# Feed-forward with Strassen products: VectorE's work reordered and paired, the convolution on one stretch, and the low part of one weight sum made by GpSimd

## The reference

```
def conv_ffn(h, p, buf):
    u = h @ p['w_ffn_up']
    a, v = u[..., :D_FF], u[..., D_FF:]          # D_FF = 2816
    T = a.shape[1]
    ext = jnp.concatenate([buf.astype(a.dtype), a], axis=1)
    w = p['ffn_conv_w']
    c = p['ffn_conv_b'] + sum(ext[:, j:j + T] * w[j] for j in range(CONV_W))   # CONV_W = 3
    out = (jax.nn.silu(c) * v) @ p['w_ffn_down']
    return out, ext[:, -(CONV_W - 1):]
```

## Time and profile before

| what | value |
|---|---|
| median of three runs | 1988.31 us |
| the profiled execution | 1987.89 us, of which the span is 1986.1 us |
| PE busy | 1825.2 us (92%) |
| DVE busy | 1313.5 us (66%) |
| ACT busy | 962.6 us (48%) |
| POOL busy | 242.9 us (12%) |
| mean granted clock of PE | 0.985 |

### The profile page before, as it was taken

One profiled execution on the slowest core, in us unless ns is written; L12 is line 12 of the kernel. 1 busy time (PEld: TensorE's weight loads), 2 busy tenths in 40 slices (PEclk: granted clock), 3 DMA queues, 4 the chain that ended last, 5 costly groups with the idle time before them and its releaser, 6 DMA issues.

```text
span 1986.1 us, 31514 instructions
## 1 busy us (share of the span) xinstructions
PE 1825.2 (92%) x11636; PEld 1658.3 (83%) x11636; DVE 1313.5 (66%) x2229; ACT 962.6 (48%) x1601; POOL 242.9 (12%) x261
## 2 busy tenths in 40 slices
PE   8999999998889999898899999999988989898985
PEld 7999965798888889897799999658988989798974
DVE  5777865437675666677777778653575675757776
ACT  6444455437544343535654444653555353534345
POOL 0000034001111111111000001430011111111100
PEclk9999999999899999999999999999999999999998
DMA  5211231411646565555131123132135556555621
GB/s 189 72 55 66 68 89 46 131 54 49 152 123 138 144 145 131 133 154 123 43 107 55 52 72 80 63 118 68 65 84 132 133 131 150 131 140 150 139 69 59
DMA packets 98713, 203.71 MB, mean 103 GB/s; under 512 B 16800, under 2 KB 35616, under 8 KB 98536
## 3 DMA queue, kind: packets, MB, share of 16 engines
q1 hardware_dynamic: 63760, 144.06, 22.6%
q0 software_dynamic: 21888, 39.86, 12.3%
q10 hardware_dynamic: 12912, 17.78, 2.7%
HBM read 170.65 MB, written 8.65 MB: 90 GB/s over the span
## 4 chain that ended last, share of the span: by engine, by line
PE 58%; DVE 21%; ACT 10%; DMA 5%; issue 4%; DVEq 0%; POOL 0%; ACTq 0%; SPq 0%; POOLq 0%
PE G L768 36%; PE WA L768 12%; PE WB L768 8%; DVE tmp L2100 6%; DVE wlo L2100 4%; ACT tmp L1453 3%; DMA t<-in_wstream 3%; DVE ax L2100 2%; DVE Y L2100 2%; DMA wraw<-in_wstream 1%; PE G L772 1%; ACT sq L1453 1%; DVE gl L2100 1%; ACT Y L1453 1%; PE WB L772 1%
## 5 line engine op out<-in xcount | busy, mean ns | idle before, releaser
L768 PE MATMUL G<-Hh,wlo 128*128 128x328 f32 x1384 | 456.8, 330 | 56.5 <-DVE p L2100 32.5
L768 PE MATMUL G<-Hh,whi 128*128 128x328 f32 x1384 | 436.8, 316 | 0.0
L768 PE MATMUL G<-Hl,whi 128*128 128x328 f32 x1384 | 435.8, 315 | 0.0
L768 PEld LDWEIGHTS G<-Hh,wlo 128*128 128x128 f32 x1384 | 264.3, 191 | 76.5 <-DVE p L2100 40.2
L768 PEld LDWEIGHTS G<-Hh,whi 128*128 128x128 f32 x1384 | 264.6, 191 | 2.3 <-issue 0.4
L768 PEld LDWEIGHTS G<-Hl,whi 128*128 128x128 f32 x1384 | 263.8, 191 | 0.0
L1453 ACT ACTIVATE whi<-wraw 128x1024 fp32r<-128x1024 f32 (+2 forms) x194 | 160.3, 826 | 184.2 <-PE G L768 113.2
L2100 DVE TENSOR_TENSOR wlo<-wraw,whi 128x1024 fp32r<-128x1024 f32 (+2 forms) x194 | 181.7, 936 | 45.1 <-ACT whi L1453 28.2
L768 PE MATMUL G<-gh,wlo 128*128 128x328 f32 x424 | 136.1, 321 | 23.5 <-DVE tmp L2100 17.1
L2100 DVE SCALAR_TENSOR_TENSOR tmp<-ax,cols,tmp 128x528 f32<-128x528 f32 (+1 forms) x176 | 98.6, 560 | 57.9 <-ACT tmp L1453 51.8
L768 PE MATMUL G<-gh,whi 128*128 128x328 f32 x424 | 134.5, 317 | 0.0
(11 more groups left out here) (326 smaller groups left out, 4135.1 us busy)
## 6 DMA issues: line engine op xcount, KB each, us to landing
wraw<-in_wstream SPq DMA_DIRECT2D x108, 512.0 KB, 3.3
wff<-in_wstream SPq DMA_DIRECT2D x40, 512.0 KB, 4.7
t<-in_wstream SPq DMA_DIRECT2D x76, 256.0 KB, 4.1
t<-in_wstream POOLq DMA_DIRECT2D x38, 256.0 KB, 5.5
ckT<-in_ckT SPq DMA_DIRECT2D x12, 512.0 KB, 3.4
wff<-in_wstream POOLq DMA_DIRECT2D x20, 256.0 KB, 4.2
t<-wff POOLq DMA_DIRECT2D x20, 256.0 KB, 3.3
wff<-t POOLq DMA_DIRECT2D x20, 256.0 KB, 3.3
```

The source lines that it names most:

```text
L768: return pe.matmul(out, lhsT, rhs, start=start, stop=stop, skip_group_check=True)
```

## The change

- The order of splits: `LATE` is changed, and where two units in neighbouring places are split behind the same product (`PAIRS`: B11 with B21, T2 with T3, T4 with B22), ACT and DVE do both in one instruction of 1024 columns. `t2` and `t3` become one tensor `t23` for that. `ring` is as before, so some pairs stay two instructions.
- The low part of T1 is made by POOL (`t1_low`), behind `sum_t4` of its chunk and ahead of `sum_t1` of the next. It has its own semaphore, `t1_split`; `split_sem` tells PE and SP which of the two to wait for.
- The convolution works in its own tensor `cc` on one stretch of 672 columns with one instruction per tap. The silu now goes from `cc` to `tmp` in two. `cc` takes the place of `cos4`, which is loaded again in layer 1. `halo` and `carry` go from DVE to ACT.
- In a chunk, DVE does `conv_rest` ahead of most splits, and splits T2 with T3 of the next chunk ahead of the addition to `u2`, which leads to `ax`.
- The first stage of the feed-forward: `token_sums` of POOL is gone; the sums are made by DVE (20 instructions of 328 columns, `s_sum`) and ACT in `Sf`. The weights of the fifth and sixth tile are split earlier; part of the sums, and the high part of the last of them, move behind the start of the first down pass.
- The end of a layer: the first weights of the next layer are split before the last halves, and the second halves of outputs 3 and 4 come behind the first residuals.

```
-LATE = {B11: 0, B21: 0, T2: 2, T3: 1, T1: 1, T4: 1, B22: 0}
+LATE = {B11: 1, B21: 0, T2: 1, T3: 0, T1: 0, T4: 1, B22: 0}
+PAIRS = (B11, T2, T4)
...
+        def pair_of(g):
+            k = product_of(g % UNITS_L)
+            return k is not None and k[1] in PAIRS and ring[g + 1] == ring[g] + 1 and \
+                any(g % UNITS_L in v and g % UNITS_L + 1 in v for v in split_after.values())
+        def split_at(g):
+            l, u = divmod(g, UNITS_L)
+            before = l * NS + sum(u0 + T1 <= u for u0 in U_PROD.values())
+            return ("t1_split", before) if by_pool(g) else ("w_split", g + 1 - before)
...
@@ POOL
+            def t1_low(l, c):
+                g = unit_of(chunk_no(l, c), T1)
+                pool.wait_ge(S("w_hi"), g + 1)
+                pool.tensor_tensor(w_lo_of(g), raw_unit(g), w_hi_of(g), ALU.subtract).then_inc(S("t1_split"), 1)
...
-                token_sums(l)
                 sum_t1(l, NPL)
                 sum_t2(l, NPL)
                 for c in range(NPL, KF):
                     sum_t3(l, c)
                     sum_t4(l, c)
+                    t1_low(l, c)
                     if c + 1 < KF:
                         sum_t1(l, c + 1)
                         sum_t2(l, c + 1)
@@ ACT
                 def conv_first(c):
-                    act.wait_ge(S("conv"), 2 * k + 1)
...
-                    step(f(d[:, 0:PT], s_[:, 0:PT], ACT.Identity, **kw))
-                    did(f(samples(d[:, PT:T]), samples(s_[:, 2 + PT:EXT], DT + 2)[:, :, 0:DT], ACT.Identity, **kw), "silu")
+                    act.wait_ge(S("ax"), l * KF + c + 1)
+                    did(f(cc[:, 0:EXT - 2], ax[:, c % 2, 0:EXT - 2], ACT.Identity, scale=cols[:, l, C_CW + c:C_CW + c + 1],
+                          bias=cols[:, l, C_CB + c:C_CB + c + 1]), "silu")
...
@@ ACT, first down pass
                     for n in range(KD):
                         if not q:
                             act.wait_ge(S("down"), down_no(l, q, n))
-                            act.wait_ge(S("s_dve"), s_split(l, 1 if n < KH else 3))
                             did(f(two(Y[:, n, :]), halves(down_bank(n)), ACT.Copy), "act_took")
+                        if not q and n == 3:
+                            s_high(Sh[:, 0, :, :], Sf[:, 0, :, :], 18)
+                            act.wait_ge(S("tile"), t0 + T_UP + 2 * NPL)
+                            for x in range(2):
+                                s_high(Hh[:, 2 * x:2 * x + 2, cols_of(1)], s4_part(x), 12, -1.0)
@@ DVE, chunk
+                    lows(l, u0 - 2)
                     if pending is not None:
                         conv_rest(pending)
-                    lows(l, u0 - 2)
-                    halo(c)
-                    lows(l, u0 - 1)
+                    lows(l, u0 + B11)
                     after(B21)
...
-                    lows(l, u0 + B11)
                     if pending is not None:
                         times_v(pending)
-                    lows(l, u0 + B21)
+                    lows(l, u0 + T2)
                     if pending is not None:
                         g_low(pending)
-                    lows(l, u0 + T2)
                     after(T1)
                     did(tt_(p7[:, :], p7[:, :], bank(G[s], 0), ALU.add), "dve_took")
-                    lows(l, u0 + T3)
+                    lows(l, u0 + T1)
                     after(T4)
...
-                    carry(c)
-                    lows(l, u0 + T1)
@@ DVE, end of a layer
                 split_to[0] = 0
+                w_low(l + 1, 0)
...
-                for n in (3, 4):
-                    ffn_out_b(n)
-                for n in (3, 4):
-                    add_square_b(n0 + N_FFNPOST, n)
+                ffn_out_b(3)
                 dve.wait_ge(S("rstd_a"), 2 * l + 2)
```

More of the change, by code:

```diff
@@ L609, in _ @@
                 if earlier[g] is not None:
-                    sp.wait_ge(S("w_split"), earlier[g] // PIECES * UNITS_L + last_unit(earlier[g] % PIECES) + 1)
+                    last = earlier[g] // PIECES * UNITS_L + last_unit(earlier[g] % PIECES)
+                    sp.wait_ge(*split_sem(last))
+                    if product_of(last % UNITS_L) and product_of(last % UNITS_L)[1] == B22:
+                        sp.wait_ge(*split_sem(last - B22 + T1))
                 if p == P_CHUNK[NPL]:
@@ L1539, in _, with w_high_two @@
             split_to = [0]
+            def w_high_two(l, u):
+                g = l * UNITS_L + u
+                for v in (g, g + 1):
+                    act.wait_ge(S(raw_ready(v)[0]), raw_ready(v)[1])
+                    for w in users[v]:
+                        act.wait_ge(S(unit_end(w)[0]), unit_end(w)[1])
+                did(f(pair_in(whi, g), raw_pair(g), ACT.Copy), "w_hi", by=2)
             def highs(l, u):
@@ L1931, in chunk @@
                         silu(pending)
+                    halo(c)
                     highs(l, u0 + B21)
@@ L1935, in chunk @@
                     highs(l, u0 + T2)
+                    if pending is not None:
+                        g_high(pending)
                     after(T3)
@@ L1938, in chunk @@
                     did(f(p7[:, :], bank(WA, s), ACT.Copy), "act_took")
-                    if pending is not None:
-                        g_high(pending)
-                    highs(l, u0 + T3)
                     highs(l, u0 + T1)
@@ L2052, in _ @@
                     square(0, 1)
+                    for n in (3, 4):
+                        ffn_out_b(n)
+                        scale_y(n, 1)
                     ffn_out_b(KD - 3)
@@ L2696, in _ @@
                 for k in range(KH):
-                    did(stt(Y[:, KH + k, cols_of(0)], Y[:, KH + k, cols_of(0)], weight(KH + k), Y[:, k, cols_of(0)],
-                            ALU.mult, ALU.add), "s_dve")
-                s_low(0, Sl[:, 1, :, :], Sh[:, 1, :, :], 0, 1, -1.0)
+                    s_sum(Sf[:, 1, k, :], KH + k, 1, Sf[:, 2, k, :], True)
                 plain_v(1)
+                plain_a(2)
                 w_low(l, P_UP + 6)
                 g_low(1)
+                conv_rest(2)
@@ L2703, in _ @@
+                plain_v(2)
+                w_low(l, P_UP + 7)
                 for k in range(KH):
-                    did(stt(Y[:, KH + k, cols_of(1)], X[:, KH + k, cols_of(1)], weight(KH + k), Y[:, KH + k, cols_of(1)],
-                            ALU.mult, ALU.subtract), "s_dve")
-                s_low(1, Sl[:, 2, :, :], Sh[:, 2, :, :], 0, 0)
-                plain_a(2)
-                w_low(l, P_UP + 7)
-                conv_rest(2)
-                s_low(2, Sl[:, 0, :, :], Sh[:, 0, :, :], 1, 1)
```

250 lines of the change are left out of this document (147 added, 103 removed).

## The result

The forecast was wrong: no gain. The changed kernel takes 1993.38 us (median of 20 runs), the kernel before beside it 1989.87 (20 runs); ratio 1.0018, 95% interval 1.001 to 1.0026. The forecast was 1930 us. The profiled execution of after spans 1987.4 us, that of before 1986.1.

The account below looks back on a forecast made before the run. The prediction took PE's chunk waits, from a ring through DVE, as the main bound, with smaller waits in the first stage and between layers: 1987.9 - 36.0 - 18.2 - 3.0 - 1.0 = 1929.7, so 1930 us, range 1898 to 1966.

Parts of the forecast that it names:

- the term of the chunks: Feed-forward chunks: PE's waits cost 31.7 instead of 49.7 us per layer, 36.0 us saved in two layers.
- the ring through POOL: Chunks: T3 landed, ACT's and DVE's pair, POOL's subtraction, next sums, T3 landing again: 14.5 us per chunk, 1.85 above 12.65.
- the landing of T3: Chunks: T3's sum lands 5.5 us after its issue, the old median; bounds 3.7 and 7.5.
- 12.65 + 3.0: Second chunk of a group: seven products of 12.65 us in all, plus waits of 3.0 at T2 and T4.
- rival (a): Chunks: the sums keep up, T3's landing in some 4 us, ring 13 us: 1891 us in all; chance 0.18.
- sign of being wrong: PE's chunk waits below 20 or above 45 us per layer, or the first stage saving less than 5.
- the first stage: Start of each layer's feed-forward: chunk 3 starts at 526.5 instead of 535.6, 9.1 us saved, 18.2 in two layers.
- Rival (c): Chunks: POOL's subtraction held by DVE, the sums slip, ring 17.8 us (decides from 17.0): slower, 2011 us; chance 0.08.
- Rival (b): Chunks gain nothing: the late pair ahead of `ax` costs what DVE was spared, 3.55 us per chunk stays: 1966 us; chance 0.20.
- From layer 0 to 1: Layer change: the wait of 4.1 us becomes 1.6 for the second weight; 3.0 us saved, bounds 0 and 6.
- The end, -1.0: End of layer 1: the norm's factor comes about 2.6 us earlier, 1.7 us of work moves behind it; 1.0 saved.
- The shared port: DVE and POOL lock each other out, so POOL's subtraction follows DVE's pair: ring 14.5 us, without the lock 13.8.

Follow-up runs that it names:

- e1: The changed kernel with T1's low part back on DVE instead of POOL: 1937.65 us, ratio 0.9726.
- e2: The kernel before with only T1's low part added to POOL's queue behind `sum_t4`: 2045.09 us, ratio 1.0267.
- e9: The changed kernel with T1's low part on DVE, no pairs and the old LATE: 1901.47 us, ratio 0.9559.
- e4: The changed kernel with POOL's low part of T1 moved between the next chunk's sums of T1 and T2 (same group): 1954.24 us, ratio 0.9816.
- e10: The changed kernel, T1's low part still on POOL, without pairs and with the old LATE: 1966.97 us, ratio 0.9882.

## Why the prediction was wrong

The step that failed is the term of the chunks, -36.0 us: measured +11.9 and +6.1, 54 us off. The parts were named rightly: the ring through POOL sets the distance of the chunks, T2 waits for the copy `p1`, B22's waits are gone, ACT's pair is released by the DMA on `t`. The term of the ring that was mis-sized is the landing of T3. Over the 18 rounds that lie wholly within a group the ring is, in the mean: from the pair to T1's sum 3.46 us (forecast 1.1 + 1.3 + 1.2); T1's to T2's sum 4.69 (4.5); T2's to T3's 0.55 (0.9); from T3's sum to the next pair 7.83, of which 7.64 are the landing (5.5, upper bound 7.5); together 16.5, forecast 14.5. The distance between starts of T2 is 16.4 there: 1.9 us too much in 18 chunks, 34 us. Towards the second chunk of a group it is 16.86 where 12.65 + 3.0 was forecast: 12 us in 10 chunks. There the distance from T1's to T2's sum was mis-sized: 5.9 us in the mean, not 4.5 (in the group shown 696.19 to 702.57). The last 8 us lie outside the distances of T2; where, apart from some 3 us of the clock (below), stays open.

Why T3 lands late is not settled. It stands 0.54 us behind T2's sum every time now, and the prediction had held that very row against rival (a) and then took the old median. But the distance alone does not do it: in the kernel before, 11 of the 38 were issued 0.54 us behind T2's too, and landed in 4.7 to 6.7 us; the 27 others took 3.8 to 7.5. What the long ones have beside them is traffic. These windows are three landings in one group (5.2, 8.6 and 6.1 us); columns: length, POOL busy, clock, DMA share, GB/s.

```profile
703.10:708.50 5.40, 2.08 (x3) 1.00 0.76 132
717.16:726.00 8.84, 2.08 (x3) 0.95 0.90 227
734.90:741.20 6.30, 2.08 (x3) 0.99 0.96 201
```

T3 of the third chunk of a group has the longest landing before (6.3 us in the mean) and after (7.9). No run varies the loads beside it.

The second thing missing was the clock: the prediction counted a wait at its length and 0.23 us, but the product behind the wait shown takes 3.37 instead of 1.80 us, 1.57 more. PE's waits from chunk 3 to the last pass of layer 0 sum to 46.5 us, before to 46.1, so the 11.9 us by which the stage is longer lie in the slow products (half of 37 us), less what fewer waits save. Yet the slow products are no cost that can be added to the ring. Where the ring sets the distance, they come out of the next wait: 12.65 + 0.23 + 1.57 + the wait of 3.02 is 17.47, the distance from one T2 to the next. They cost time where no such wait follows, behind the last T2 of a group: two of the five in layer 0, some 3 us by my estimate, and none in layer 1. Nor is a long wait always followed by a slow product. This one, in layer 1, has a product of 1.93 us behind it:

```profile
1876.66 0.42 PE L820 MATMUL G<-Sh,wlo 128*128 128x328 f32 x1 [3.39 <-ACT R L1505]
...
1878.59 0.31 PE L820 MATMUL WA<-Sh,wlo 128*128 128x328 f32 x1
```

Neither sign of being wrong that the prediction gave for itself came true: PE's waits in the chunks of layer 0 are 42 us (536 to 947 us), below its bound of 45, and the first stage saves 8.9. They asked for the waits and not for the distance of the chunks, which it had given as 14 to 15 us.

Rival (c), POOL's place in the ring, is the one that came closest: the distances, 16.4 and 16.9 us, lie just under its threshold of 17.0, and e1 and e2 show that this place costs 53 to 58 us. Its reason was wrong: the subtraction takes 1.6 us and is not held by several of DVE's instructions. Its price is that the sums behind it stand while it waits for ACT's high part of T1; the prediction had that wait in its ring, but nothing in it compared the ring with one without POOL's part. Rival (b) was half right: the late pair and LATE cost 33 us (e1 against e9). The two together, some 91 us, ate what the rest brought: after without either has ratio 0.9559, 88 us less than before. The prediction had no rival for parts of such size that cancel, as it costed the pairs as DVE time saved (0.26 us each) and not as a part that waits for its partner.

The other terms: the first stage is right in layer 0 (chunk 3 at 526.66, forecast 526.5; the wait of 4.92 for ACT's copy to `Y` stands where it was put):

```profile
523.29 0.57 PE L820 MATMUL WB<-gh,wlo 128*128 128x328 f32 x1 [4.92 <-ACT Y L1505]
```

From layer 0 to 1, -3.0 was forecast; the waits of the earlier trace rows became 1.92 and 3.03, the second a new one, and the 8.9 us saved up to chunk 3 of layer 1 are no more than the first stage alone saved in layer 0:

```profile
984.56 0.42 PE L820 MATMUL G<-Hh,wlo 128*128 128x328 f32 x1 [1.92 <-DVE wlo L2183]
991.22 1.46 PE L820 MATMUL WA<-sq,ones 128*128 128x328 f32 x2 [3.03 <-ACT sq L1505]
```

The end, -1.0, is +1.1. The durations held: a tap of 672 columns 0.919 (0.92), ACT's 0.95 (0.95), `halo` and `carry` 0.22 (0.25). In a chunk with a pending one DVE is busy 10.4 instead of 11.9 us with 15 or 16 instead of 23 instructions, which with 0.1 us between two is the 2.3 us less that were worked out; the time was not saved where the chunk waits. The shared port, which the prediction took from the Trainium skill (SBUF — State Buffer, "SBUF: two separate sides"), shows again: `ax` in two pieces beside POOL took 1.04 us where the same pieces alone, in e1, took

```profile
712.72 0.69 DVE L2182 TENSOR_TENSOR ax<-R 128x200 f32<-128x200 f32 x2
```

It is 0.35 us, and not what decides between after and e4, which has the same subtraction and is 40 us faster.

## What to carry to other kernels

Before work is moved to an engine that is idle, read what it issues next: a queue that starts transfers is on the path however little it is busy (GpSimd 14%). The work put into it holds the transfers behind it for its own time, here 1.3 to 2.0 us, and for its wait for an operand, here up to 11.5 us. A pair of operands is ready when its later one is; count that wait before the instruction saved. And a change made of parts is tried part by part: here +58 and +33 hid -88.

## What the runs showed of the hardware

An accumulating transfer of 256 KB issued by GpSimd (the sum of T3) landed 4.6 to 9.2 us after its issue, median 6.5, where it took 3.7 to 7.5 before, median 5.5. The shortest distance to the one ahead of it, 0.54 us, goes with 4.6 to 9.2 us and so does not fix it; the landing of 8.6 us lay beside 227 GB/s, that of 5.2 beside 132.

GpSimd's subtraction of 512 columns takes 1.29 us where it starts first (694.95), and 1.61 or 1.98 where it starts during an instruction of DVE with two operands in SBUF (710.44; 724.96 in e10).

TensorE, idle for 4.05 us after a stretch at 2.4 GHz, went on at 1.2 GHz for the 12 matmuls of a product. In layer 0 all 11 waits from 2.3 us on had this behind them and the three shorter ones ahead of T2 had not. It is no rule of one wait: in layer 1 the waits of 2.38 and 3.39 us had full speed behind them. In the kernel before none of the waits of layer 0 (up to 2.1 us) had it, but one of 1.77 us in layer 1 (at 1913.31) did.
